# Second block of a two-block transformer kernel: attention outputs kept with features on partitions, norms scaled after the output projection

## The reference, cut to what matters

```python
def second_block(x, ...):                       # x: 512 x 1024
    h = rmsnorm(x, attn_norm_g)
    fq, fk, fv, f_logit, sq, sk, sv = split(h @ w_in)      # each 512 wide; f_logit 8 wide
    o_fox = fox_attention(fq, fk, fv, log_sigmoid(f_logit + forget_bias))   # 8 heads of 64
    o_sb = stick_breaking_attention(sq, sk, sv)                             # 8 heads of 64
    o = concat([rmsnorm(merge_heads(o_fox), fox_out_g),    # norm over 512 features
                rmsnorm(merge_heads(o_sb), sb_out_g)])     # norm over 512 features
    x = x + o @ w_out
    h = rmsnorm(x, ffn_norm_g)
    u = causal_dwconv(h @ w_up, conv_w, conv_b)
    gate, val = split(u)
    x = x + (silu(gate) * val) @ w_down
    return rmsnorm(x, final_norm_g)

# fox:   softmax over s <= t of  q_t.k_s/8 + F[t] - F[s],  F = cumsum(log_f)
# stick: A[t,s] = sigmoid(z[t,s]) * prod_{s<j<t} (1 - sigmoid(z[t,j])), s < t, z = q.k/8
```

## Time and profile before

| | us |
|---|---|
| median of three runs | 1698.64 |
| profiled execution, its own time | 1700.36 |
| its span | 1698.5 |
| PE busy | 1633.2 (96%) |
| DVE busy | 883.5 (52%) |
| ACT busy | 645.4 (38%) |
| POOL busy | 366.1 (22%) |
| chain that ended last: PE | 83% of the span |
| chain that ended last: DVE, POOL, ACT | 6%, 5%, 3% |

### The profile page before, as it was taken

The page is one execution under the profiler, slowest core; times in us unless marked ns, Lnnn a source line. Parts: engine busy times, 40 slices in busy tenths (PEclk is TensorE's granted clock), DMA queues, the critical chain, the costliest instruction groups (busy, mean ns, idle before and its releaser), DMA issues.

```text
span 1698.5 us, 19241 instructions
## 1 busy us (share of the span) xinstructions
PE 1633.2 (96%) x7582; PEld 1292.9 (76%) x7582; DVE 883.5 (52%) x1401; ACT 645.4 (38%) x1106; POOL 366.1 (22%) x318
## 2 busy tenths in 40 slices
PE   5999998988999999999999999998999999999998
PEld 3566787766767788888888887775788888888886
DVE  5446555366357555444343324587564767777222
ACT  4332223355445433333322212466563444444222
POOL 3444214364012116111110205033202400000000
PEclk9999998999999999999999999999999999999999
DMA  6121112211221323233333322321102232332322
GB/s 231 51 74 37 50 55 75 87 57 56 75 63 50 112 88 98 92 95 99 99 100 94 94 98 70 112 63 38 44 7 76 86 98 90 97 99 87 124 88 73
DMA packets 39221, 139.51 MB, mean 82 GB/s; under 512 B 4331, under 2 KB 4971, under 8 KB 38940
## 3 DMA queue, kind: packets, MB, share of 16 engines
q1 hardware_dynamic: 39132, 138.29, 25.3%
HBM read 136.14 MB, written 2.10 MB: 81 GB/s over the span
## 4 chain that ended last, share of the span: by engine, by line
PE 83%; DVE 6%; POOL 5%; ACT 3%; issue 3%; DMA 1%; SPq 0%; POOLq 0%; DVEq 0%; ACTq 0%
PE ps L387 80%; PE ps L390 3%; POOL sqs L2105 2%; POOL sqt L2103 1%; DVE raw L1056 1%; ACT whi L1489 1%; DVE W L1307 0%; DVE wlo L863 0%; DVE T L1089 0%; DMA wraw<-in_ws 0%; DMA x<-in_x 0%; POOL Lb L2158 0%; DVE tp L1051 0%; DVE sd L962 0%; DVE raw L1043 0%
## 5 line engine op out<-in xcount | busy, mean ns | idle before, releaser
L863 DVE TENSOR_TENSOR wlo<-wraw,whi 128x1024 fp32r<-128x1024 f32 (+2 forms) x220 | 271.8, 1240 | 442.7 <-ACT whi L1489 442.0
L387 PE MATMUL ps<-hThi,whi 128*128 128x512 f32 x1128 | 455.0, 403 | 1.6 <-DVE skT L1394 0.9
L387 PE MATMUL ps<-hThi,wlo 128*128 128x512 f32 x1128 | 441.5, 391 | 0.0
L387 PE MATMUL ps<-hTlo,whi 128*128 128x512 f32 x1128 | 440.9, 391 | 0.0
L1489 ACT ACTIVATE whi<-wraw 128x1024 fp32r<-128x1024 f32 (+2 forms) x244 | 251.9, 1037 | 481.9 <-PE ps L387 467.9
L387 PEld LDWEIGHTS ps<-hThi,whi 128*128 128x128 f32 x1128 | 212.9, 189 | 57.5 <-issue 16.2
L387 PEld LDWEIGHTS ps<-hTlo,whi 128*128 128x128 f32 x1128 | 213.0, 189 | 45.5 <-issue 3.6
L387 PEld LDWEIGHTS ps<-hThi,wlo 128*128 128x128 f32 x1128 | 212.6, 188 | 45.3
L387 PE MATMUL ps<-whi,hThi 128*128 128x512 f32 (+1 forms) x224 | 90.1, 402 | 6.8 <-DVE wlo L863 6.8
L387 PE MATMUL ps<-whi,hTlo 128*128 128x512 f32 (+1 forms) x224 | 85.9, 383 | 0.0
L387 PE MATMUL ps<-wlo,hThi 128*128 128x512 f32 (+1 forms) x224 | 85.8, 383 | 0.0
(11 more groups left out here) (323 smaller groups left out, 2605.7 us busy)
## 6 DMA issues: line engine op xcount, KB each, us to landing
wraw<-in_ws SPq DMA_DIRECT2D x236, 512.0 KB, 3.5
x<-in_x SPq DMA_DIRECT2D x4, 512.0 KB, 7.5
x<-in_x SPq DMA_DIRECT2D x1, 2048.0 KB, 8.4
out<-ys SPq DMA_DIRECT2D x8, 256.0 KB, 2.2
dec<-in_dec SPq DMA_DIRECT2D x1, 1024.0 KB, 15.9
wraw<-in_ws SPq DMA_DIRECT2D x4, 256.0 KB, 2.6
vec<-in_vec SPq DMA_DIRECT2D x1, 788.0 KB, 4.7
w<-in_w SPq DMA_DIRECT2D x1, 512.0 KB, 14.3
```

The lines of the kernel that those rows point to most:

```text
L387: return t.matmul(o, l, r, start=first, stop=last)
L863: v.tensor_tensor(wlo[h][:, 0:width(i)], wraw[h][:, 0:width(i)], whi[h][:, 0:width(i)].bitcast(F32), ALU.subtract).then_inc(lo_done[h], 1)
```

## The change

It does six things.

1. The product with the values is turned round: 64 columns of `sv` or `fv` are held on PE and the 128 query columns of `PT` are moved. Two heads of a pair go to the two column halves of PE (output partitions 0 to 63 and 64 to 127 of bank 7), as the first block's `window()` does it before and after. The units are reordered so that a pair of heads runs through n = 3, 2, 1, 0, for both attentions; after eight units bank 7 holds 128 features x 512 tokens.
2. The eight `out_norm` rounds go. For each pair of heads ACT takes `ohi` and a square from bank 7 (`head_high`), DVE takes `olo` (`head_low`, one 128 x 512 operation), and POOL adds up squares (`head_sums`). Roots are spread over the partitions by `head_squares` and `head_roots` (PE), once per attention.
3. `xs` and `xf` no longer share a sum: each is multiplied on DVE by its own root tile `Ro` and added to `xT` (two operations per block, where one per block was done after `xf` alone).
4. fox divides by the row sum before the transpose, per unit (DVE: a reciprocal and a multiplication of up to 128 x 512), and no longer once per n. Its scores use banks 4 and 5, its transposes bank 6.
5. The rates: `fq` 4, `fk` 4, `fv` 4, `xs` 8, `xf` 4. The stick steps so stand beside `sv`, `fq` and `fk`, one in `fv`; five fox steps in `fv`, the rest beside `xs`; the fox roots beside `xf`.
6. `x_back` uses transposes in place of products, ahead of the first weight product of its bank and not after the first slot.

Semaphores are merged (`in_inv` into `in_tab`, `in_res` into `in_x[0]`, `w_y` into `n_row`) with the same waits.

```diff
-    s_units = [(n, h) for n in (3, 0, 2, 1) for h in range(8)]
-    pairs = [(n, h) for two in ((3, 0), (2, 1)) for h in range(8) for n in two]
+
+    s_units = [(n, h) for j in range(4) for n in (3, 2, 1, 0) for h in (2 * j, 2 * j + 1)]
...
-                if s == 1 and beside:
+                if s == 0 and beside:
...
-        def out_norm_turn(q, bank):
-            w.wait_ge(o_sc, 3 * q + 3)
+        def head_squares(c, bank):
+
+            w.wait_ge(z_p, 5 * c + 3)
             take(bank)
-            for k in range(4):
-                op = across(bank, k, W5[5][:, k * 128:(k + 1) * 128])
-            op.then_inc(o_tr, 1)
-            free[bank] = [(o_lo, q + 1)]
+            for i in range(4):
+                op = mm(ps[bank][:, i:i + 1], oss[c][:, i * 128:(i + 1) * 128], ones[:, 0:1], True, True)
+            op.then_inc(z_mm, 1)
+            free[bank] = [(z_row, 2 * c + 1)]
+
+        def head_roots(c, bank):
+            w.wait_ge(z_p, 5 * c + 5)
+            take(bank)
+            mm(ps[bank][:], ones[:], sqt[:], True, True).then_inc(z_mm, 1)
+            free[bank] = [(z_row, 2 * c + 2)]
 
         def stick():
...
             def values(u):
+
                 n, h = s_units[u]
-                w.wait_ge(s_ev, u + 1)
+                w.wait_ge(s_ev, u + 2)
                 w.wait_ge(sv_c, n + 1)
-                if h == 0:
+                if n == 3:
                     take(7)
                 for k in range(n + 1):
-                    op = mm(ps[7][:, h * 64:(h + 1) * 64], PT2[u % 2][:, k * 128:(k + 1) * 128], sv[:, k, h * 64:(h + 1) * 64],
-                            k == 0, k == n)
-                op.then_inc(s_pv, 1)
-                if h == 7:
-                    free[7] = [(o_c, u // 8 + 1)]
+                    for i in range(2):
+                        op = mm(ps[7][64 * i:64 * i + 64, n * 128:(n + 1) * 128], sv[:, k, (h + i) * 64:(h + i + 1) * 64],
+                                PT2[(u + i) % 3][:, k * 128:(k + 1) * 128], k == 0, k == n)
+                        if k == n:
+                            op.then_inc(s_pv, 1)
+                if n == 0:
+                    free[7] = [(o_lo, u // 8 + 1)]
 
             for u in range(37):
                 if 4 <= u < 36:
                     turn(u - 4)
                 if u < 32 and u % 2 == 0:
                     scores(u)
-                if u in (15, 23, 31):
-                    out_norm_turn((u - 15) // 8, 6)
-                if u >= 5:
-                    values(u - 5)
+                if u >= 6 and u % 2 == 0:
+                    values(u - 6)
                 yield
...
+                w.wait_ge(x_sh, 2 * u + 2)
+                take(6)
                 for k in range(wd // 128):
...
-            for u in range(38):
-                while u == 3 and not fox_go:
+                    for i in range(2):
+                        op = mm(ps[7][64 * i:64 * i + 64, n * 128:(n + 1) * 128], fv[:, k, (h + i) * 64:(h + i + 1) * 64],
+                                PTf[(u + i) % 4][:, k * 128:(k + 1) * 128], k == 0, k == n)
+                        if k == n:
+                            op.then_inc(x_pv, 1)
+                if n == 0:
+                    free[7] = [(o_lo, 4 + u // 8 + 1)]
+
+            for u in range(36):
+                while u == 5 and not fox_go:
                     yield
+                if 3 <= u < 35:
+                    turn(u - 3)
                 if u < 32:
                     scores(u)
-                if 3 <= u < 35:
-                    turn(u - 3)
-                if u in (7, 22, 26):
-                    out_norm_turn({7: 3, 22: 4, 26: 5}[u], 3)
-                if 5 <= u < 37:
+                if u == 5:
+                    head_squares(0, 6)
...
+        group("fq", hT, h_ready(2), lambda b: (h_v, 2 * (b // 2) + 2) if b % 2 else (h_a, 2 * (b // 2) + 2), 4)
+        group("fk", hT, h_ready(2), lambda b: (h_v, 4 + 2 * (b // 2) + 2) if b % 2 else (h_a, 4 + 2 * (b // 2) + 2), 4)
         flow.beside.append(fox())
-        group("fq", hT, h_ready(2), lambda b: (h_v, 2 * (b // 2) + 2) if b % 2 else (h_a, 2 * (b // 2) + 2), 2)
-        group("fk", hT, h_ready(2), lambda b: (h_v, 4 + 2 * (b // 2) + 2) if b % 2 else (h_a, 4 + 2 * (b // 2) + 2), 4)
         group("fv", hT, h_ready(2), lambda b: (fv_c, b + 1), 4)
         fox_go.append(True)
+        for half in range(2):
+            group("xs%d" % half, lambda k: (ohi[:, k, :], olo[:, k, :]), lambda k, b: w.wait_ge(o_lo, k + 1),
+                  lambda b: (e_s, 8 * half + 2 * b + 1), 8)
         flow.drain()
-        for half in range(2):
-            group("xs%d" % half, lambda k: (ohi[:, k, :], olo[:, k, :]), lambda k, b: w.wait_ge(o_lo, 4), lambda b: None,
-                  last=False)
-        residual("xf%d", 3, lambda k: (ohi[:, 4 + k, :], olo[:, 4 + k, :]), lambda k, b: w.wait_ge(o_lo, 8), more=True)
+        flow.beside.append(fox_norm())
+        for half in range(2):
+            group("xf%d" % half, lambda k: (ohi[:, 4 + k, :], olo[:, 4 + k, :]), lambda k, b: w.wait_ge(o_lo, 4 + k + 1),
+                  lambda b: (e_s, 16 + 4 * half + b + 1), 4)
         flow.later(2, lambda: token_squares(3, 0))
...
-                    mm(ps[bank][:, k * 128:(k + 1) * 128], xT[:, 4 * half + k, b * 128:(b + 1) * 128], ident, False, False)
+                    t.matmul(ps[bank][:, k * 128:(k + 1) * 128], xT[:, 4 * half + k, b * 128:(b + 1) * 128], ident,
+                             start=k == 0, stop=False, is_transpose=True)
...
+                    if n == 3:
+                        t = px[b % 2]
+                        w.wait_ge(z_row, 4)
+                        w.wait_ge(e_x, 16 + f - 1)
+                        v.tensor_tensor(t[:], p[:], Ro[1][:], ALU.mult).then_inc(e_s, 1)
+                        w.wait_ge(e_s, 16 + f + 1)
+                        v.tensor_tensor(xT[:, f, :], t[:], xT[:, f, :], ALU.add).then_inc(e_x, 1)
+                    else:
...
+        def head_low(q, gname):
+
             w.wait_ge(o_hi, q + 1)
-            for k in range(4):
-                op = v.scalar_tensor_tensor(olo[:, j0 + k, n * 128:(n + 1) * 128], ps[bank][:, k * 128:(k + 1) * 128], col(gname, k),
-                                            ohi[:, j0 + k, n * 128:(n + 1) * 128].bitcast(F32), ALU.mult, ALU.subtract)
-            op.then_inc(o_lo, 1)
+            w.wait_ge(o_sq, q + 1)
+            v.scalar_tensor_tensor(olo[:, q, :], ps[7][:], col(gname, q % 4), ohi[:, q, :].bitcast(F32), ALU.mult,
+                                   ALU.subtract).then_inc(o_lo, 1)
...
+            def shares(u):
+                wd, c, T = 128 * (s_units[u][0] + 1), u % 6, Tf[u % 6]
+                w.wait_ge(x_ex, u + 1)
+                v.reciprocal(st2[:, 16 + c:17 + c], st2[:, 8 + c:9 + c]).then_inc(x_sh, 1)
+                w.wait_ge(x_sh, 2 * u + 1)
+                v.tensor_scalar(T[:, 0:wd], T[:, 0:wd], st2[:, 16 + c:17 + c], None, ALU.mult).then_inc(x_sh, 1)
...
+        def projected(half):
+
+            def evac(b, p, done):
+                f, t = 4 * half + b, px[b % 2]
+                w.wait_ge(blocks, done)
+                w.wait_ge(z_row, 2)
+                if f >= 2:
+                    w.wait_ge(e_s, 2 * f - 2)
+                v.tensor_tensor(t[:], p[:], Ro[0][:], ALU.mult).then_inc(e_s, 1)
+                w.wait_ge(e_s, 2 * f + 1)
+                v.tensor_tensor(xT[:, f, :], xT[:, f, :], t[:], ALU.add).then_inc(e_s, 1)
+            return evac
 
...
+        def head_high(q, gname):
+
+            w.wait_ge(s_pv if q < 4 else x_pv, 8 * (q % 4) + 8)
+            w.wait_ge(in_late, 32)
+            a.activation(ohi[:, q, :], ps[7][:], ACT.Copy, scale=col(gname, q % 4)).then_inc(o_hi, 1)
+            if q % 4 > 1:
+                w.wait_ge(z_p, 5 * (q // 4) + q % 4 - 1)
+            dst = osq if q % 4 else oss[q // 4]
+            a.activation(dst[:], ps[7][:], ACT.Square).then_inc(o_sq, 1)
 
...
+        def head_sums(c, j):
+
+            w.wait_ge(o_sq, 4 * c + j + 1)
+            if j > 1:
+                w.wait_ge(z_p, 5 * c + j - 1)
+            g.tensor_tensor(oss[c][:], oss[c][:], osq[:], ALU.add).then_inc(z_p, 1)
+
+        def head_spread(c):
+            w.wait_ge(z_row, 2 * c + 1)
+            w.wait_ge(fv_c, 4)
+            if c:
+                w.wait_ge(z_mm, 2)
+            g.tensor_tensor(small[:, 8:12], small[:, 12:16], col("mhalf", 0, 4), ALU.pow).then_inc(z_p, 1)
+            w.wait_ge(z_p, 5 * c + 4)
+            g.tensor_tensor(sqt[:].rearrange("p (i t) -> p i t", i=4), ident.unsqueeze(1).to_broadcast([128, 4, 128]),
+                            small[:, 8:12].unsqueeze(2).to_broadcast([128, 4, 128]), ALU.mult).then_inc(z_p, 1)
 
```

292 lines of the change are left out of this document (136 added, 156 removed).

## The result

The changed kernel took 1721.78 us (median of 4 runs, 1718.05 to 1724.45) against 1698.62 us (1696.29 to 1698.65, 4 runs): a ratio of 1.0138, with a 95% interval of 1.012 to 1.0156. The forecast was 1694.6 us in a range of 1683 to 1708, so the sign was wrong and the time lies outside the range.

A forecast was written before the change was run, and what follows sets the result against it. PE, busy 96% of the span, was taken as the bound, with DVE the fuller engine in stick. Terms -1.9 - 3.5 + 4.4 - 3.0 = -4.0 us gave 1694.6 us, range 1683 to 1708.

The forecast's parts named there:

- Turned value products: Value products in both attentions: passes from 0.101 to 0.0675 us each, 5.4 us less per attention.
- Stick: Unit 0's transposes to the last stick value product: 116.3 us become 105; with dense work moved, a term of -1.9 us.
- The rest: DVE's remaining idle time in stick, besides waits for casts and `ohi`: 18 us shrink to 7 through alternating unit widths.
- Rival A: Stick: the loop through DVE keeps its holes, stick takes 115 us, time 1704, up to 1710; chance 0.26.
- fox beside the projection: fox beside `xs`: cheaper value products and dropped `out_norm` turns outweigh added work and waits, -3.5 us.
- covered: fox beside `xs`: 60 us of DVE work hidden in a stretch of some 70 us, at 85%, only just.
- rival C: fox beside `xs` is bound by DVE: 80 us in place of 70, time 1704; chance 0.15.
- The dense work behind stick: 48 dense matmuls, 10.8 us, move from stick to behind it, where PE has them beside fox.
- The clock: Transposes not counting as activity for PE's clock: given no time of its own.
- Behind it: fox roots beside `xf`, waits at squares and roots, later token squares: +4.4 us, bounds +2 and +7.
- `x_back`: Transposes in place of products: eight groups from 0.81 to 0.44 us each, -3.0 us.
- The signs named beforehand: If right: DVE 80% or more in stick, PE 97% or more from `fv` through `xf`, `sqt` wait 1 to 2 us.

The follow-up runs named there:

- e6: Changed kernel with fox drained ahead of `xs` and units in order 3, 0, 2, 1 in both attentions: 1705.64 us, ratio 1.0043 to the kernel before.
- e7: Changed kernel with only the unit order 3, 0, 2, 1 in both attentions, fox still beside `xs`: 1713.07 us, ratio 1.009 to the kernel before.
- e9: Changed kernel with unit order 3, 0, 2, 1 and the low parts of the `xs` weights made on POOL: 1710.08 us, ratio 1.0073.
- e13: e9 with all copies of fox's transposed shares (`PTf`) made by ACT: 1701.0 us, ratio 1.0023 to the kernel before.
- e14: e9 with the `xs` results added by one DVE instruction, the spread root left out of the computation: 1704.65 us, ratio 1.0041.
- e10: e7 with `fq` at two attention steps a slot in place of four: 1713.22 us, ratio 1.0087 to the kernel before.
- e17: Changed kernel with one edit, all copies of fox's transposed shares made by ACT: 1709.02 us, ratio 1.0062 to the kernel before.
- e5: Changed kernel with fox drained ahead of `xs`, then on four score banks and two transposing banks: 1709.8 us, ratio 1.0074.
- e8: Changed kernel with fox drained ahead of `xs` and the multiplication by the row sums' reciprocals left out: 1716.23 us, ratio 1.0112.
- e4: Kernel before with only `x_back` by transposes, ahead of the first weight product of its bank: 1694.51 us, ratio 0.9979.
- e15: Changed kernel, fox drained, order 3, 0, 2, 1, more banks once drained, `fq` at two, stick's copies on ACT: 1701.64 us, ratio 1.0023.

## Why the prediction was wrong, point by point

**Turned value products: right.** Sixteen passes take 1.03 us to the next start, 0.064 each (0.0675 predicted). The first and the last of these rows are the ends of the stick stretch:

```profile
1098.46 0.60 PE L394 MATMUL ps<-vec,Lb 128*128 128x128 f32 x4
1108.34 1.09 PE L391 MATMUL ps<-PT,sv 128*64 128x128 f32 x16
1109.37 0.50 PE L391 MATMUL ps<-hThi,whi 128*128 128x512 f32 x1
...
1211.50 0.44 PE L391 MATMUL ps<-PT,sv 128*64 128x128 f32 x4 [0.32 <-DVE PT L1359]
```

They were as cheap as said. What it was worth no run shows by itself; in stick and fox PE waited, so that a shorter product need not shorten the stage.

**Stick: 105 predicted, 113.0 measured, 8.0 us of the miss.** The forecast had widths 4, 4, 3, 3, 2, 2, 1, 1 leave "no long stretch of narrow units". Four narrow units in a row are such a stretch: with 3, 0, 2, 1 the time is 105.7 to 106.5 us in five executions (e6, e7, e9, e13, e14), against 110.1 to 113.4. The term that was too small is "The rest": 7 us were taken for it, and by the order the 7 to 8 us above the forecast are in it. Rival A was near in its number, 115 us at DVE's share of 75%, and its sign came: DVE is busy 84.8 of the 113 us by the four windows, and PE waits for DVE's copy. Its reason, four steps in every slot, isn't needed, as the order gave the forecast's time at the same rates; what the rates add stays open, as e10 with two steps in `fq` has 8.2 us more but also 42 dense matmuls more (9.5 us by the prediction's price).

**fox beside the projection: -3.5 predicted, and +18.5 measured. This is the step that failed.** With 10.8 for the dense work moved behind stick, the stretch to `xf` was put at 86.6 us and took 108.6. The price of DVE's work was not too low: 60 us were predicted and 48.56 measured; the sixteen operations on the blocks of `xs` and the copies to `olo` came as estimated, as these groups by form from 1230 to 1325 us show (the last answers to the earlier trace rows, one where four were):

```profile
L1436 DVE TENSOR_TENSOR xT<-xT,px 128x512 f32<-128x512 f32 x8 | 5.5, 692 | 0.3
L1434 DVE TENSOR_TENSOR px<-ps,Ro 128x512 f32<-128x512 f32 x8 | 5.5, 690 | 6.7 <-PE ps L391 6.7
...
L1305 DVE SCALAR_TENSOR_TENSOR olo<-ps,vec,ohi 128x512 fp32r<-128x512 f32 x4 | 3.0, 751 | 4.4 <-ACT osq L1840 3.0 <-ACT oss L1840 1.4
```

What was wrong is "covered": a load was set against the length of the stretch, and what stands ahead of the copy of bank 6 in DVE's queue had no term. PE's waits there were put at 1.5 us (for bank 7) and the clock at nothing; PE stood idle for 14.3 us in the window and lost 8.3 to the clock, together about the 22.0 us of the miss. The forecast's words against rival C were that fox "has no loop through four queues". It had one through three: ACT's cast, DVE's low part, `px` and `xT`, the copy, PE's transposes. Rival C came out in its number (the window of fox beside `xs` is 83.2 us where it had 80 in place of 70) but not in its cause, as DVE was 58% busy and not full. With the copies on ACT (e17) the window is 67.6 us; then the forecast was 6.4 us too low, and PE is idle for 6.9 us, 6.0 of them waiting for the copy out of the single bank. Order and casts together give 2.1 us of it (e13), which is within the spread of such times. What the single bank and the division are worth by themselves there stays open: e5 and e8 tried them with fox drained, and with the copies on ACT neither was tried.

**The dense work behind stick: about right.** The stretch ahead of `xs` grew from 12.0 us (last dense matmul of `fv` before) to 25.4, with three steps of fox in it before and five after; of the 13.4 us, 10.8 were predicted.

**The clock: given no time, and it cost.** In the forecast it was only in rival A. In the window beside `xs` it is 8.3 us by the comparison with e17. In stick the granted clock of the four windows comes to 24 us at 0.50, where the earlier trace rows gives 10; what that cost where PE also waits, no run parts.

**Behind it: right in sum, by two errors that cancel.** +4.4 predicted, +4.2 measured. The 1.3 us of waiting between squares and roots doesn't show, but the token squares wait 2.25 us longer than in the earlier trace rows, where 1.2 was predicted:

```profile
1322.97 0.94 PE L391 MATMUL ps<-ones,oss 128*128 128x1 f32 x8
1326.63 1.02 PE L391 MATMUL ps<-sqt,ones 128*128 128x512 f32 x2
...
1357.74 1.87 PE L391 MATMUL ps<-ones,sqs 128*128 128x1 f32 x8 [2.88 <-POOL sqs L2147]
```

Their own duration (1.87 in place of 1.05) and a granted clock of 0.51 from 1357 to 1364 us show what else that wait cost.

**`x_back`: right, and a little more.** -3.0 predicted. A group takes 0.35 us to the next start where the earlier trace rows has 0.81, and 8 x 0.46 is 3.7; e4 gives 2.7 to 3.6. In the table the last stage is only 0.6 shorter, as the low clock behind the squares falls into it.

```profile
1591.04 0.60 PE L876 MATMUL ps<-vec,xT 128*128 128x128 f32 x4
1591.39 0.48 PE L391 MATMUL ps<-whi,achi 128*128 128x512 f32 x1
```

**The signs named beforehand.** DVE at 80% in stick: it was 75%, a wrong sign. PE at 97% from `fv` to `xf`: it was 83% beside `xs`, the sign of C. The wait for `sqt` beside `xf` didn't come. Passes as said; `x_back` groups came 0.35 us long and not 0.45.

The sum: -4.0 predicted and about 28 us measured over the table's stages (24.1 in own times, as the first stick scores came 4.0 us earlier in this execution). Of the 32 us between them, 8.0 are stick, 22.0 fox beside `xs`, 2.4 the last stage.

## What to carry to other kernels

An engine that is half idle covers nothing if a copy on which the matmuls' next bank depends stands in its queue behind work that waits for a third engine. When two loops are laid beside each other, write down for each release of a shared bank what is queued ahead of it on its engine, and try that release on an engine whose queue has no long wait ahead of it; here sixteen copies moved were worth 15.6 us of a stage in fox, while in stick ACT's copies (e15) gave nothing. Order units so that narrow ones don't follow each other in a long row, and count a hole twice, as the clock may go with it.
